# Branch products of a hybrid encoder layer: five gate tiles in flight, four pairs of PSUM banks, later splits

## What is computed

```
gate = jax.nn.sigmoid(proj[..., OFF_GATE:])
merged = (gate[..., :D_MODEL] * (ya @ lp['w_branch_a'])
          + gate[..., D_MODEL:] * (ob @ lp['w_branch_b']))
return merged @ lp['w_mix_out'], ...
```

## Time and profile before

| what | us |
|---|---|
| median of 3 runs | 3438.36 |
| the runs | 3425.46, 3438.82, 3438.36 |
| time of the profiled execution | 3429.22 |
| its span, first to last instruction | 3427.4 |
| PE busy in it | 3252.5 (95%) |
| first and last matmul with a result of the b halves and later jobs | 1995.50 to 2108.79 |

### The profile page before, as it was taken

How to read it: one execution, slowest core, us unless ns; L and a number is a source line. 1 busy time by engine, 2 the same in 40 slices (tenths; PEclk the granted TensorE clock), 3 DMA queues, 4 the chain that set the end, 5 groups by cost and what they waited for, 6 DMA issues and landing times. The chain is left out here.

```text
span 3427.4 us, 50204 instructions
## 1 busy us (share of the span) xinstructions
PE 3252.5 (95%) x19977; PEld 3084.9 (90%) x19977; DVE 1311.5 (38%) x2296; ACT 682.2 (20%) x1325; POOL 955.2 (28%) x436
## 2 busy tenths in 40 slices
PE   6999999999999999999998979999799999999998
PEld 4999999999879888888797979978699999999997
DVE  3232332333446655554343364322225233233324
ACT  5100000000133333433333332133311000000001
POOL 3434333333322222111202123221133333333331
PEclk9999999999999999999999989999899999999999
DMA  5311111111133133111111144033401111111111
GB/s 190 137 37 43 49 37 43 43 43 37 55 146 126 54 127 135 74 61 41 65 71 66 50 148 154 31 107 137 149 31 44 50 43 43 40 39 43 37 49 56
DMA packets 96554, 251.06 MB, mean 73 GB/s; under 512 B 11808, under 2 KB 53536, under 8 KB 93728
## 3 DMA queue, kind: packets, MB, share of 16 engines
q1 hardware_dynamic: 47632, 149.51, 13.2%
q10 hardware_dynamic: 48784, 99.55, 8.0%
HBM read 199.05 MB, written 49.97 MB: 73 GB/s over the span
## 5 line engine op out<-in xcount | busy, mean ns | idle before, releaser
L131 POOL TENSOR_TENSOR w_hi<-w_raw,zero 128x1024 fp32r<-128x1024 f32 x199 | 383.1, 1925 | 2159.0 <-PE psum L164 1316.1
L164 PE MATMUL psum<-x_hi,w_hi 128*128 128x384 f32 x2928 | 578.6, 337 | 44.0 <-DVE e_m L2541 18.2
L164 PE MATMUL psum<-x_lo,w_hi 128*128 128x384 f32 x2928 | 575.1, 336 | 0.0
L164 PE MATMUL psum<-x_hi,w_lo 128*128 128x384 f32 x2928 | 571.4, 335 | 0.0
L164 PEld LDWEIGHTS psum<-x_hi,w_hi 128*128 128x128 f32 x2928 | 515.2, 189 | 55.4 <-issue 36.6
L164 PEld LDWEIGHTS psum<-x_lo,w_hi 128*128 128x128 f32 x2928 | 516.7, 189 | 1.9
L164 PEld LDWEIGHTS psum<-x_hi,w_lo 128*128 128x128 f32 x2928 | 514.9, 188 | 0.0
L134 POOL TENSOR_TENSOR w_lo<-w_raw,w_hi 128x1024 fp32r<-128x1024 f32 x199 | 492.1, 2473 | 15.7
L416 DVE TENSOR_TENSOR f_hid<-psum,f_gate 128x384 f32<-128x384 f32 x132 | 73.6, 558 | 858.3 <-PE psum L164 855.9
L366 ACT ACTIVATE f_gate<-psum 128x384 f32<-128x384 f32 x132 | 64.8, 493 | 1478.2 <-PE psum L164 1474.5
L164 PE MATMUL psum<-f_h_hi,w_hi 128*128 128x384 f32 x1056 | 269.5, 336 | 0.0
(11 more groups left out here) (296 smaller groups left out, 3374.8 us busy)
## 6 DMA issues: line engine op xcount, KB each, us to landing
w_raw<-units SPq DMA_DIRECT2D x224, 512.0 KB, 3.6
gate_dram<-b_stash ACTq DMA_DIRECT2D x48, 192.0 KB, 1.9
e_gate<-gate_dram ACTq DMA_DIRECT2D x48, 192.0 KB, 2.5
a_kc<-k_cache ACTq DMA_DIRECT2D x4, 2048.0 KB, 7.8
a_vc<-v_cache ACTq DMA_DIRECT2D x4, 2048.0 KB, 13.0
x_sk<-mem_k ACTq DMA_DIRECT2D x8, 1024.0 KB, 8.6
proj_dram<-a_cv ACTq DMA_DIRECT2D x12, 576.0 KB, 2.7
b_pad<-proj_dram SPq DMA_DIRECT2D x12, 576.0 KB, 4.8
```

Of the source, the lines that this page charges most:

```text
L131: pool.tensor_tensor(k.w_hi[s][:, :], k.w_raw[s][:, :], k.zero[:, 0:1].to_broadcast([P, D]), ALU.add)\
L164: mm = pe.matmul(out, wl if part == 2 else wh, (xl if part == 1 else xh)[:, n0:n1], start=(part == 0 and i == 0), stop=(part == 2 and i == ...
```

## The change

Four things change, all in `merge_phase`.

1. Gates: three more buffers (`early_gates`, in memory of the lower output that is not yet written). The gates of jobs 0 to 4 are loaded at once at the start, ten DMAs instead of four, ahead of everything else in ACT's list; step 0 then loads job 6, step 1 job 5, steps 2 to 4 load nothing, and from step 5 the loads go two jobs ahead as before. The sigmoid of job 0 moves behind the splits of third 1.
2. Banks: from job 6 on, four pairs of banks are used in turn. Job 6 waits for job 1 (before: 5), jobs 7, 8, 9 for jobs 4, 5, 5, and a job from 10 on for the job four before it.
3. DVE: the subtraction of job j stands behind the sum of job j+1 (`rest`).
4. The second splits of thirds 0 and 1 of `ya` move from steps 4 and 5 to steps 6 and 7 on ACT and on DVE. The split of third 2 moves from step 2 to step 1 on ACT, that of `ob` third 2 from step 3 to step 2.

```diff
+    two_gates = pair("e_gate0", 512), pair("e_gate1", 9216)
+    early_gates = [pair(f"e_gate{2 + e}", 8 * THIRD * e - 16 * T) for e in range(3)]
...
-    AHEAD = (0, 1, 3, 4, 2, 5)
-    FRONT = len(AHEAD)
-    a_bank = dict(zip(AHEAD, (4, 5, 6, 7, 0, 1)))
+    FRONT = 6
+    HALVES = ((0, 0), (1, 0), (3, 0), (4, 0), (2, 0), (5, 0), (0, 1), (1, 1), (2, 1), (3, 1), (4, 1), (5, 1))
+    A_BANK, PAIRS = (4, 5, 0, 6, 7, 1), ((4, 5), (6, 7), (0, 1), (2, 3))
+    USERS = {6: 1, 7: 4, 8: 5, 9: 5}
+    EARLY = 5
...
-        return (a_bank[j], 2 + j % 2) if j < FRONT else (2 * (j % 2), 2 * (j % 2) + 1)
+        return (A_BANK[j], 2 + j % 2) if j < FRONT else PAIRS[(j - FRONT) % 4]
...
-            pe.wait_ge(k.merged.sem, k.merged.at(j + 2 if j == FRONT else j + 1))
-            if j >= FRONT:
-                half(j, 0, part(n, 0))
+
+            last_user = USERS[j] if j < FRONT + 4 else j - 4
+            pe.wait_ge(k.merged.sem, k.merged.at(last_user + 3))
+            half(j, 0, part(n, 0))
             half(j, 1, part(n, 1))
...
-        load(0)
-        load(1)
+        for j in range(EARLY):
+            load(j)
         upper_b(0)
         upper_last(0)
-        gates(0)
         upper_b(1)
         upper_last(1)
+        gates(0)
         act.wait_ge(k.s_out.sem, k.s_out.at(48))
         for j in range(JOBS):
+            if j == 1:
+                upper_a(2)
             if j == 2:
-                upper_a(2)
-            if j == RING:
                 upper_b(2)
                 upper_last(2)
-            if j in (4, 5):
-                upper_a(j - 4)
+            if j in (6, 7):
+                upper_a(j - 6)
             if j + 1 < JOBS:
                 gates(j + 1)
             act.wait_ge(k.merged.sem, k.merged.at(j + 1 + 2))
             act.activation(chunk(hi, j), m1[:, j % 2, :], ACT.Copy).then_inc(k.merged_hi.sem, 1)
-            if j + 2 < JOBS:
+            if j < 2:
+                load(6 - j)
+            elif j >= EARLY and j + 2 < JOBS:
                 load(j + 2)
...
+        def rest(j):
+
+            dve.wait_ge(k.merged_hi.sem, k.merged_hi.at(j + 1))
+            dve.tensor_tensor(chunk(lo, j), m1[:, j % 2, :], chunk(hi, j).bitcast(F32), ALU.subtract)\
+                .then_inc(k.merged_split.sem, 1)
...
-            if j in (4, 5):
-                lower(slice(0, 4), j - 4, y_raw[:, 0:4, third(j - 4)], 4 + j)
+            if j in (6, 7):
+                lower(slice(0, 4), j - 6, y_raw[:, 0:4, third(j - 6)], 2 + j)
...
             dve.tensor_tensor(m1[:, j % 2, :], a1[:, j % 2, :], b1[:, j % 2, :], ALU.add).then_inc(k.merged.sem, 1)
-            dve.wait_ge(k.merged_hi.sem, k.merged_hi.at(j + 1))
-            dve.tensor_tensor(chunk(lo, j), m1[:, j % 2, :], chunk(hi, j).bitcast(F32), ALU.subtract)\
-                .then_inc(k.merged_split.sem, 1)
+            if j >= 1:
+                rest(j - 1)
+        rest(JOBS - 1)
```

More of the change, by code:

```diff
@@ L754, in __init__ @@
         self.yb_landed = [self.third_landed[1][1], *self.x_landed[0:2]]
+        self.early_gate = self.x_landed[2:5]
         self.q_moved, self.streams_loaded = self.counter("q_moved"), self.counter("streams_loaded")
@@ L2380, in pair @@
         return nc.alloc_sbuf_tensor_at(name, [P, 2, THIRD], F32, offset=work + at)
-    gt = pair("e_gate0", 512), pair("e_gate1", 9216)
+    two_gates = pair("e_gate0", 512), pair("e_gate1", 9216)
+    early_gates = [pair(f"e_gate{2 + e}", 8 * THIRD * e - 16 * T) for e in range(3)]
     b1, m1, a1 = pair("e_b", 6144), pair("e_m", 12288), pair("e_a", 15360)
@@ L2394, in banks, with gate @@
     def banks(j):
-        return (a_bank[j], 2 + j % 2) if j < FRONT else (2 * (j % 2), 2 * (j % 2) + 1)
+        return (A_BANK[j], 2 + j % 2) if j < FRONT else PAIRS[(j - FRONT) % 4]
     def done(j):
-        return FRONT + j + 1 if j < FRONT else 2 * j + 2
+        return HALVES.index((j, 1)) + 1 if j < FRONT else 2 * j + 2
+    def gate(j):
+        return early_gates[j - 2] if 2 <= j < EARLY else two_gates[j % 2]
     def chunk(a, j):
@@ L2433, in tensor @@
         pe.wait_ge(k.o_copied.sem, k.o_copied.at(0))
-        for j in AHEAD:
+        for j, ab in HALVES:
             m, n = order[j]
[L2436 to L2446, removed]
+            if ab == 0:
+                if n == 0:
+                    pe.wait_ge(k.unit_split.sem, k.unit_split.at(m + 1))
+                if m == 0:
+                    pe.wait_ge(k.third_split.sem, k.third_split.at(n + 1))
+                if banks(j)[0] < 2:
+                    pe.wait_ge(k.evacuated.sem, k.evacuated.at(2))
+                half(j, 0, branch.chunks(n))
+            else:
+                if m == 0:
+                    pe.wait_ge(k.lned.sem, k.lned.at(0))
+                    pe.wait_ge(k.third_split.sem, k.third_split.at(2 * n + 4))
+                pe.wait_ge(k.merged.sem, k.merged.at(j + 1))
+                half(j, 1, part(n, 1))
+        for j in range(FRONT, JOBS):
+            m, n = order[j]
             if j == FRONT:
@@ L2462, in load, with landed @@
             for ab in range(2):
-                act.dma_start(gt[j % 2][:, ab, :], k.gate_dram[8 * ab + m][:, n * THIRD:(n + 1) * THIRD])\
-                    .then_inc(k.kv_slot[j % 2].sem, 16)
+                act.dma_start(gate(j)[:, ab, :], k.gate_dram[8 * ab + m][:, third(n)]).then_inc(landed(j).sem, 16)
+        def landed(j):
+            return k.early_gate[j - 2] if 2 <= j < EARLY else k.kv_slot[j % 2]
         def gates(j):
-            act.wait_ge(k.kv_slot[j % 2].sem, k.kv_slot[j % 2].at(32 * (j // 2) + 32 + 32))
-            act.activation(gt[j % 2][:, :, :], gt[j % 2][:, :, :], ACT.Sigmoid).then_inc(k.gate_sigmoid.sem, 1)
+            if 2 <= j < EARLY:
+                act.wait_ge(landed(j).sem, landed(j).at(32))
+            else:
+                loads = j // 2 if j < 2 else (j - 3 if j % 2 else j - 4) // 2
+                act.wait_ge(landed(j).sem, landed(j).at(32 * loads + 32 + 32))
+            act.activation(gate(j)[:, :, :], gate(j)[:, :, :], ACT.Sigmoid).then_inc(k.gate_sigmoid.sem, 1)
         def upper_a(n):
@@ L2534, in vector @@
             dve.wait_ge(k.gate_sigmoid.sem, k.gate_sigmoid.at(j + 1))
-            dve.tensor_tensor(a1[:, j % 2, :], pa[:, 0:THIRD], gt[j % 2][:, 0, :], ALU.mult)
-            dve.tensor_tensor(b1[:, j % 2, :], pb[:, 0:THIRD], gt[j % 2][:, 1, :], ALU.mult)\
+            dve.tensor_tensor(a1[:, j % 2, :], pa[:, 0:THIRD], gate(j)[:, 0, :], ALU.mult)
+            dve.tensor_tensor(b1[:, j % 2, :], pb[:, 0:THIRD], gate(j)[:, 1, :], ALU.mult)\
                 .then_inc(k.gated.sem, 1)
@@ L2556, in merge_phase @@
     for b in range(2):
-        k.kv_slot[b].base += 16 * JOBS
+        k.kv_slot[b].base += 32 * sum(1 for j in range(JOBS) if j % 2 == b and not 2 <= j < EARLY)
+    for early in k.early_gate:
+        early.base += 32
     return stage
```

## The result

| what | before | changed |
|---|---|---|
| median of 7 runs each, us | 3433.74 | 3413.36 |
| lowest to highest | 3424.79 to 3438.82 | 3409.40 to 3417.09 |
| profiled execution: time, span | 3429.22, 3427.4 | 3413.36, 3411.6 |
| PE's granted clock, mean over the span | 0.982 | 0.985 |

The ratio is 0.9947, with a 95% interval of 0.9936 to 0.9958: about 18.2 us faster (14.4 to 22.0 by the interval), just over half a per cent; the medians themselves differ by 20.4 us. The forecast was 18.7 us. Its absolute number, 3419.7, was 6.3 us too high, and 4.6 of that is the median of before, which seven runs put at 3433.74 and three had put at 3438.36. The measured median lies in the range.

The account below looks back on a forecast made before the run. PE, busy 95% of the span, was taken as the bound, with 25.7 us of loss; less stalls of 1.8, 1.5, 1.7 and 2.0, 18.7 us saved, taking the median from 3438.36 to 3419.7 us, range 3405 to 3431.

Parts of the forecast that it names:

- The bound and the loss: Merge stage: only PE's stalls and slow matmuls can be won, 25.7 us: 18.2 waits, 6.5 clock, 1.0 restarts.
- First stall: Ahead of the b halves: six more gate issues at 0.46 us each delay the first split; PE stands 1.8 us.
- Job 0: Start of stage: moved sigmoid hidden by the b half, merged 0 at 2001.2; a table-load drain would cost 1.1 us.
- Gates: Jobs 1 to 4: sigmoids no longer follow their own load; six extra tiles land by some 2002.5, in time.
- B half 4 and 5: PE ahead of these halves waits for merged 2 and merged 3: stalls of 1.5 and 1.7 us.
- Job 9: PE waits for third 1's second split, DVE starting 0.2 us ahead of POOL: stall of 2.0 us.
- A: Rival at job 9: POOL wins the race, job 9 starts 2.3 us later, clock costs 2.6, median 3424.6; chance 0.17.
- B: Rival at the start: 0.98 us per issue, first stall 4.9 us and clock loss, median 3425.4; chance 0.13.
- C: Rival: POOL and DVE collide less, job 9 does not stall, 20.7 us saved, median 3417.7; chance 0.08.
- D: Rival from job 9 on: gate refill becomes the bound, 23 us slower, 3461; decides from a 4.0 us wait; chance 0.03.
- E: Rival: sigmoids still wait for own loads, PE for the job two before; nothing won, 3438; chance 0.04.
- none of the stalls reaches 3.3 us, so the clock stays: PE's clock in the stage: a 3.3 us stretch without matmuls had left it at 1.00, so 1.00 throughout.

Follow-up runs that it names:

- v_first: Changed kernel with the loads of gates 2, 3 and 4 behind the splits of thirds 0 and 1: stage 106.3 us, time 3416.65 us.
- v_waits: Changed kernel with job 9 waiting only for third 0's second split and job 10 for third 1's: stage 104.7 us, time 3417.19 us.
- u_banks: Changed kernel with two pairs of banks from job 6 on instead of four: stage 112.1 us, time 3414.90 us.
- v_late: Changed kernel with both DVE splits of third 2 at step 4, job 6's b half waiting for the last: stage 116.8 us, time 3425.66 us.
- race_lost: Changed kernel with one extra ACT copy ahead of third 0's second upper split, so POOL starts before DVE: stage 113.2 us, time 3421.06 us.
- u_second: Changed kernel with the second splits of thirds 0 and 1 back at steps 4 and 5: stage 109.7 us, time 3414.10 us.
- u_rest: Changed kernel with each subtraction directly behind its own sum: stage 113.0 us, time 3421.80 us.
- v_fw2_early: Changed kernel with gate loads 2-4 later, job 0's sigmoid between first splits, job 9's wait loosened, second splits at steps 4, 5: stage 106.6 us, ratio 0.9949.

## Why the prediction was right

Point by point, in the stage's own length:

- **The bound and the loss.** That only PE's stalls and slow matmuls count, and that they were 25.7 us, held. The sum of it now: 1.16 at the start, 4.23 of waits, 0.99 of restarts, 6.4 in all, where 7.0 were forecast. 25.7 - 6.4 = 19.3, the measured saving of the stage. That the whole time agrees to 0.5 us (18.2 against 18.7) says less: its interval is 14.4 to 22.0 us.
- **First stall, forecast 1.8.** The b halves began 1.16 us later against the stage's start. Two sizes were off, one against the other. An issue took more than the 0.46 taken:

```profile
1991.57 5.30 ACTq L2477 DMA_DIRECT2D e_gate<-gate_dram  x10
1996.92 1.17 ACT L2499 ACTIVATE x_hi<-y_raw 128x1152 fp32r<-128x1152 f32 x1 [8.80 <-DMA e_gate<-gate_dram]
```

  5.30 / 10 is 0.53. But the issues began 5.5 us into the stage, not 6.7 as before. This start is the least certain number of the stage: in seven other profiles with the same ten issues in front it lay between 5.1 and 6.6 us, and the first stall between 1.0 and 2.9. In four of these eight profiles it was 1.0 to 1.1 us, in the other four 1.98 to 2.92, with a fallen clock behind it. Both profiles of the changed kernel are of the better half, and no run shows how often it would fall in the other.
- **Job 0.** Its sum was forecast 18.5 us into the stage; ACT's copy of it began at 18.2 (2004.26). The moved sigmoid was hidden by the b half but for 0.2 us: the b half of job 0 ended at 2002.37, and `e_a`, which comes 0.04 us behind PE at job 1, began at 2002.61, released by the gate. The table load took 1.28 us again, and the sigmoids began 0.01 us behind it:

```profile
2000.37 1.28 ACT L2489 ACT_TABLE_LOAD   x1
2001.66 1.58 ACT L2489 ACTIVATE e_gate<-e_gate 128x768 f32<-128x768 f32 x2
```

  ACT was idle for 0.02 us ahead of it, so no drain shows; the 2.66 us per switch of the Trainium skill (ScalarE: Activation LUTs, "What ACT_TABLE_LOAD costs") do not show either, and the measurement decides.
- **Gates.** The sigmoids of jobs 1 to 4 started without a wait for data, as forecast. The turns between the queues, which the Trainium skill describes (DMA: Bandwidth & Descriptors, "Queues, rings and completion order"), cost nothing for the third that they were feared for: the upper split of `ob` third 2 ran at 2007.67 straight behind the copy. The rule is seen in the rates, 61.5% of the engines' time for SP's queue and 44.3% for ACT's between 1994 and 1998 us (packets overlap, so the sum is over 100), but moving six tiles behind the first splits landed the next raw third only 0.5 us sooner (12.7 us into the stage in the changed kernel, where its split started at 1998.77, and 12.2 in v_first). Even that is within the scatter: with the same ten issues in front, this split ran without a wait at 12.3 us in v_waits and waited until 13.1 in u_banks.
- **B half 4 and 5, forecast 1.5 and 1.7.** Waits of 1.25 and 1.35 and 0.33 for each restart: 1.6 and 1.7. What keeps them alive is named by v_late: the two splits of third 2 on DVE.
- **Job 9, forecast 2.0.** 1.63 + 0.33 = 2.0. DVE won the race by 0.17 us where 0.2 was forecast, and POOL's operation ended 1.76 us behind DVE's, the number read off. The step ahead of it was wrong about the work: the forecast said that job 9 needs the second split of third 1, and v_waits shows that only the code's wait did. The 2.0 us came out because that wait is in the changed kernel.
- **From job 9 on.** 15 jobs in 62.4 us: from 2030.18 to 2092.86 are 62.7.
- **Rivals.** A did not occur and was priced right for the stall (2.3 against 2.35) and too high for the clock (2.6 against about 1.5), as race_lost shows. B occurred in part: issues of 0.53, not 0.98. C's mechanism, no stall at job 9, was reached by v_waits with another edit. D did not occur: ACT waited 2.1 us on average for a gate (36.4 / 17), under the 4.0 at which it would decide. E did not occur: PE's waits for `e_m` fell from 18.2 to 2.6 us.

**Where the reasoning was lucky.** The step "none of the stalls reaches 3.3 us, so the clock stays" gave the right clock for the changed kernel by a rule that the experiments contradict. In three versions the first stall was 2.0 to 2.1 us, in v_late 2.92, and the clock fell behind it. The stretch of u_second before, in and behind it:

```profile
1990.00:1995.00 5.00, 4.89 (x29) 4.57 (x27) 0.06 (x1) 1.26 (x2) 0.00 (x0) 1.00 1.05 375
1995.00:1997.00 2.00, 0.13 (x1) 0.16 (x2) 2.00 (x3) 1.98 (x4) 0.00 (x0) 1.00 1.07 386
1997.00:2001.00 4.00, 4.00 (x15) 4.00 (x16) 1.72 (x3) 2.66 (x3) 0.00 (x0) 0.57 1.06 372
```

15 matmuls in 4.0 us cost 1.4 us more than at full clock. A first stall of 1.0 to 1.1 us had no such effect in four profiles. With the stall of 1.8 that I forecast, the clock might have fallen; the forecast of 1.00 then rested on a row that could not carry it.

**What is not settled.** How the four parts share the 19.3 us: undone one at a time they cost 5.3, 10.0, 6.3 and 2.9 us, 24.5 together, and clock and start blur the last two. What moves the start of ACT's first issue between 5.1 and 6.6 us was not tried.

## What to carry to other kernels

Where a loop's step issues a load, waits for it and only then serves the bottleneck's consumer, first take the waits out of the first round, where nothing has been buffered yet; undoing the gates loaded ahead alone gave back 10 us of the 19. Before moving work between engines that exclude each other, count how many such operations of the one are still to come when the other starts: here each lasted as long as the other engine's turn, not its own length. And ask of each semaphore wait what the job reads, since a wait one count too strict cost 2 us that a changed number took away.

## What the hardware showed that I had not expected

- **A short stall can cost more than itself, and its length alone does not decide.** A stall of 1.98, 2.04 or 2.08 us ahead of the b halves was followed by 0.57 over four us, that is by 1.2 GHz for most of it. So was one of 2.92 there by 0.67 (v_late), and one of 2.21 at b half 4 by 0.63 (u_rest). One of 2.11 us at job 8 (u_second, v_fw2_early) and one of 3.3 at the stage's end left 1.00; one of 3.98 at job 9 (race_lost) and one of 2.88 there (u_banks) did not. What else decides is open.
- **DVE and POOL exclude each other operation by operation, to the favour of neither,** where DVE's has both inputs in SBUF. Whoever is first keeps its time (1.76, 1.89); the other pays the first one's remainder: POOL 3.35 instead of 1.89, DVE 3.26 instead of 1.76, a 384-wide subtraction up to 2.76 instead of 0.55. DVE's operations that read psum are not held up (0.54 to 0.56).
- **Untouched code differs between executions by more than the edit is worth.** The stage began at 1974.5 us and at 1986.1 us in two profiles of the same kernel, 11.6 us apart, while its own length agreed to 0.01 us. Four versions on one chip, with the same code ahead of the stage, reached it at 1979.5 to 1986.1 us, so it is not only the chip. For edits of a few us the length of the stage is the measure, and the whole time needs many rounds.
